# Issuing the 16 copies of the first weight sums together instead of one per weight piece

## What the kernel computes

```python
h = rmsnorm(x, norm_w)
gq, gk, gv, gg, glr, hq, hf, hi, hg = split(h @ w_in)        # w_in: 2048 x 7184
log_a = log_sigmoid(glr @ gla_w_up + gla_b_up) / 16           # glr: 16 low-rank columns
o_a = head_rmsnorm(gla(gq, gk, gv, log_a)) * silu(gg)         # 4 heads
f = lb + (1 - lb) * sigmoid(hf)
o_b = head_rmsnorm(gla(hq, 1 - f, hi, log(f))) * silu(hg)     # 8 heads
x = x + concat(o_a, o_b) @ w_out                              # w_out: 2048 x 2048
return rmsnorm(x, final_norm_w)
```

## Time and profile before

| | |
|---|---|
| median of 3 runs | 866.5 us |
| profiled execution, its own time | 865.74 us |
| its span, first to last instruction | 864.0 us |
| PE busy | 851.8 us, 99% |
| DVE / ACT / GpSimd busy | 591.8 / 424.6 / 85.1 us |
| chain that ended last | PE 89%, DVE 5%, ACT 4% |
| moved by DMA | 167.75 MB, 194 GB/s on average |
| copies of the first sums (L549) | 16, issued 37.67 to 116.6 us |
| adds of the first sums (L557) | 16, issued 122.3 us to about 200 us |

### The profile page before, as it was taken

One profiled execution on the slowest core, in us unless ns is written; L12 is line 12 of the kernel. 1 busy time (PEld: TensorE's weight loads), 2 busy tenths in 40 slices (PEclk: granted clock), 3 DMA queues, 4 the chain that ended last, 5 costly groups with the idle time before them and its releaser, 6 DMA issues.

```text
span 864.0 us, 13755 instructions
## 1 busy us (share of the span) xinstructions
PE 851.8 (99%) x5365; PEld 697.9 (81%) x5365; DVE 591.8 (68%) x949; ACT 424.6 (49%) x594; POOL 85.1 (10%) x128
## 2 busy tenths in 40 slices
PE   8999999999999999999999999999999999999996
PEld 5887888888888888888888878888888888888885
DVE  6733476653587747577887878889885678556766
ACT  7521532324444435274565665855655465335454
POOL 4110111110000001011111100000111100000000
PEclk9999999999999999999999999999999999999999
DMA  8286679988764856568776655545777987856654
GB/s 335 65 267 195 175 203 223 203 196 241 232 185 144 274 168 198 170 175 178 151 169 147 146 177 181 166 146 158 161 170 153 283 224 263 293 196 194 195 171 195
DMA packets 75459, 167.75 MB, mean 194 GB/s; under 512 B 7365, under 2 KB 15593, under 8 KB 74505
## 3 DMA queue, kind: packets, MB, share of 16 engines
q1 hardware_dynamic: 45554, 108.02, 38.2%
q0 software_dynamic: 16896, 50.34, 27.2%
q10 hardware_dynamic: 12952, 8.61, 3.4%
HBM read 158.56 MB, written 58.72 MB: 251 GB/s over the span
## 4 chain that ended last, share of the span: by engine, by line
PE 89%; DVE 5%; ACT 4%; issue 1%; ACTq 0%; DMA 0%; DVEq 0%
PE main L577 54%; PE main L837 8%; PE main L773 5%; PE sc L837 4%; PE st L837 2%; PE po L837 2%; PE sc L630 2%; PE po L658 2%; PE st L643 1%; PE st L773 1%; PE po L773 1%; PE sc L773 1%; PE po L661 1%; PE main L689 1%; DVE w_lo L1295 1%
## 5 line engine op out<-in xcount | busy, mean ns | idle before, releaser
L577 PE MATMUL main<-h_hi,w_hi 128*128 128x512 f32 x640 | 254.2, 397 | 0.1
L577 PE MATMUL main<-h_hi,w_lo 128*128 128x512 f32 x640 | 249.7, 390 | 0.0
L577 PE MATMUL main<-h_lo,w_hi 128*128 128x512 f32 x640 | 249.3, 389 | 0.0
L1295 DVE TENSOR_TENSOR w_lo<-raw,w_hi 128x1024 fp32r<-128x1024 f32 x100 | 122.1, 1221 | 113.1 <-ACT w_hi L885 112.4
L885 ACT ACTIVATE w_hi<-raw 128x1024 fp32r<-128x1024 f32 x100 | 105.7, 1058 | 180.8 <-PE main L577 135.7
L577 PEld LDWEIGHTS main<-h_hi,w_lo 128*128 128x128 f32 x640 | 120.1, 188 | 25.8
L577 PEld LDWEIGHTS main<-h_hi,w_hi 128*128 128x128 f32 x640 | 120.2, 188 | 25.5 <-issue 0.5
L577 PEld LDWEIGHTS main<-h_lo,w_hi 128*128 128x128 f32 x640 | 120.3, 188 | 23.6
L907 ACT ACTIVATE ex<-ex 128x512 f32<-128x512 f32 (+2 forms) x84 | 52.5, 641 | 23.4 <-DVE ex L1432 15.1
L577 PE MATMUL main<-w_hi,h_hi 128*128 128x512 f32 x128 | 50.9, 398 | 0.0
L1772 DVE TENSOR_TENSOR w_lo<-feat,w_hi 128x1024 fp32r<-128x1024 f32 x26 | 31.8, 1225 | 27.1 <-ACT w_hi L1218 26.9
(11 more groups left out here) (314 smaller groups left out, 1496.3 us busy)
## 6 DMA issues: line engine op xcount, KB each, us to landing
raw<-in_w_in SPq DMA_DIRECT2D x102, 512.0 KB, 4.7
w_sum<-in_w_out POOLq DMA_DIRECT2D x48, 512.0 KB, 5.3
w_sum<-in_w_in POOLq DMA_DIRECT2D x24, 512.0 KB, 5.8
w_sum<-w_sum POOLq DMA_DIRECT2D x24, 512.0 KB, 5.8
raw<-w_sum SPq DMA_DIRECT2D x24, 512.0 KB, 4.3
feat<-w_sum SPq DMA_DIRECT2D x24, 512.0 KB, 4.3
raw<-in_w_out SPq DMA_DIRECT2D x14, 512.0 KB, 5.1
feat<-in_w_out SPq DMA_DIRECT2D x10, 512.0 KB, 4.7
```

What stands on the lines that cost most here:

```text
L577: mm = pe.matmul(main[c][:, :], a, b, start=(k == 0 and j == 0), stop=(k == KT - 1 and j == 2))
L1295: dve.tensor_tensor(w_lo[:, q % SPL, :, :], (first_raw if first else raw)[:, q % RAW, :, :], w_hi[:, q % SPL, :, :], ALU.subtract).then_in ...
```

## The change

The copies of pair 2 no longer call `pace()`. Before them GpSimd waits once, until four low parts have been made (`SPL` is 4). The copies of the other pairs and all adds still call it; the counter `paced[0]` begins at 1 and is advanced by `pace()` alone.

```diff
             for pair in (2, 0, 1):
                 if pair == 0:
                     paced[0] = D_N + ND
+                if pair == 2:
+                    pool.wait_ge(lo_ok, SPL)
                 for j, (name, source) in enumerate(COPIED):
                     for q in range(QP):
-                        pace()
+                        if pair != 2:
+                            pace()
                         pool.dma_start(w_sum[pair, j, q], weight_piece(pair, source, q)).then_inc(
                             w_copied[pair * len(XS) + j], 16)
```

## The result

The median after is 880.0 us (878.62 to 880.78, five runs); before, on the same chip, 866.3 us (865.61 to 866.57). The ratio is 1.0157, 95% interval 1.0146 to 1.0167: slower by 13.7 us. The forecast was 873.3 with a range up to 879.0. The direction was right; the loss was twice the forecast and lies outside the range. Two executions behind the numbers further down, one of e2 (1063 us) and one of the kernel before beside e9 and e10 (1217 us), ran at a mean granted clock of 0.75 and 0.66 and are left out of every ratio and of e2's median.

The account below looks back on a forecast made before the run. PE was taken as the bound, so only new waits could change the time: 865.74 us of the profiled execution + 5.3 + 1.5 = 872.5, or 873.3 against the median of the runs; range 866.0 to 879.0.

Parts of the forecast that it names:

- What bounds the kernel: PE, busy 851.8 of 864.0 us; lighter DMA gives nothing back, so only making PE wait changes the time.
- The copies: GpSimd issues 16 copies from 18.9 to 29.3 us; each takes 1.5 us, with 1.3 and 1.68 as ends.
- (a): x tiles and first weights beside the copies after 20.25 us: 1.5 us of work, cover over 10 us, costs nothing.
- (b): Low-rank columns, one small packet per copy packet, land at 49.2 us; PE waits 5.3 us before piece 5, high end 7.9.
- my first rival: Same as "nothing waits": small packets go in bunches, columns land by 43.9 us, time 866.5 us; chance 0.23.
- (c): PE's clock falls to 1.2 GHz behind the wait before piece 5: costs 1.5 us, low end 0, high end 3.
- (d): Weight loads of pieces 6 and 7 after that wait, beside adds: just fit, cost nothing; high end 2.7 us.
- (e): Adds end near 120 us instead of 200, lightening a stretch where PE did not wait: gains nothing.
- nothing waits: Rival: small packets go in bunches, low-rank columns land by 43.9 us, PE unaffected, 866.5 us; chance 0.23.
- order of issue: Rival: engines serve first issued first; columns land at 35.2 us, loads of pieces 6 and 7 late, 875.3 us; chance 0.18.
- Both: Rival on slow engines: (b) at 7.9, (c) at 3, (d) at 2.7 us, giving 880 us; chance 0.04.

Follow-up runs that it names:

- e2: Changed kernel, but GpSimd starts the 16 copies only when the low-rank columns and gla_w_up have landed, adds still early: 873.2 us.
- e9: Changed kernel, but SP loads the low-rank columns ahead of the copies and the adds keep their earlier pace (pieces 17 to 32): 866.78 us.
- e10: Changed kernel, but ACT issues gla_w_up and four parameters only behind the rounding of the low-rank columns, and adds keep their earlier pace: 879.35 us.
- e11: As e10, but ACT's six issues (gla_w_up and parameters) stand further back, inside group(0, ...) at its sixth piece: 876.30 us.
- e4: Changed kernel, but the 16 adds are paced by pieces 17 to 32 as in the kernel before; copies as changed: 876.17 us.
- e8: Changed kernel, but half of the low-rank columns left out, their buffer filled by 128 runs of 512 bytes; 72 packets per DMA engine: 877.08 us.
- e3: Changed kernel, but 128 runs of 1 KB from w_in replace the 2048 of 64 bytes, low-rank columns left out; adds early: 872.29 us.

## Why the prediction was wrong

**What bounds the kernel:** right. PE was full; only new waits could change the time, and all the loss is waits and clock.

**The copies:** issued from 19.34 to 30.4 (forecast 18.9 to 29.3). In 28 to 40 us they moved 3.54 MB, 0.524 / 3.54 x 12 = 1.78 us each beside the small packets, slower than my upper end of 1.68.

**(a) x and the first weights:** nothing, right. The weight load that I put beside the columns did not go out before 50.0 in after, as PE was late.

**(b) The low-rank columns:** the mechanism held, one small packet for one large. The Trainium skill's rule ("DMA: Bandwidth & Descriptors", section "SWDGE vs HWDGE vs iDMA") of packets with up to 64 descriptors, which was my first rival, is again not what the trace shows: 894 against 971 packets in 28 to 40 us. The landing was right too, 50.5 for 49.2. It was right by parts that cancel, which is luck: the first of these packets moved near 28.9 us, not 25.0 (3.9 later), no weight load came between (1.5 less), and the 128 turns took 21.6 us where I had 22.7 with their own work (1.1 less). **The step that failed** is the path from the columns to PE: I looked only at who waits for the columns, L1031, and had PE wait 5.3 us for `w_lo` ahead of piece 5. I had not followed what else ACT issues on the same queue behind them: L1020 stood for 13.26 us, and held the transposes for 8.0 us before anyone wanted the columns. I had put down that the standing work on ACT was the high half of piece 5; it was the high parts of x, which come first. In e11, with that out of the way, (b) alone is 8.0 us against my 5.3, and 7.9 was its high end.

**(c) The clock:** right in kind, 2.0 us for 1.5, but it fell twice, the second time after a wait of only 2.1 us.

**(d) The later weight loads, "just fit", costed at nothing:** wrong by 3.8 us (e4). Landings of 8.8 and 9.5 us against the 8.3 that I took as worst. And I compared each low part with the time at which PE wants that piece, not with what stands behind it on DVE: the banks for piece 8 waited behind the low part of piece 9. The high end that I gave it, 2.7 us, was too small: four adds in 5 us are 13 us of work for all engines by the earlier trace rows, which the text noted and did not set against these loads.

**(e) Later relief:** nothing, right.

In us: forecast 5.3 + 1.5 + 0; measured 8.0 + 2.0 + 3.8, and 0.4 in small waits. The 5.3 and the 8.0 are not the same wait. Of the rivals, "nothing waits" fell with the ratio of the packets, and "order of issue" with the landing: it had the columns at 35.2 us, and they came at 50.5. The stretch that spoke for it, 124.5 to 127.5 us before, also has 87 packets of ACT's queue beside the add's 192, which the prediction did not say; so it did not show that issue order rules. "Both", which allowed for (b), (c) and (d) at their high ends at once, gave 880, with a chance of 0.04. That it has the measured time is luck: its 7.9 is the wait at piece 5, which after does not have, and its 2.7 a wait for piece 7, where PE waited for a bank. But its kind is right in this, that the terms go up together: all three hang on full DMA queues.

## What to carry to other kernels

When a burst is put in front of a queue of small descriptors, do not only ask who waits for their data; ask also what the issuing engine issues next on that queue, and what stands behind that instruction. A pacing counter that is taken from one kind of transfer changes the pace of all others that share it: price these first. For a late operand, compare its time with the next thing behind it in its engine's order, not only with its own consumer.

## What the runs showed that was not expected

- **An issue that stands.** ACT's next DMA issue on its queue took 13.26 us with 128 packets a DMA engine ahead of it and the queue hardly moving; it ended when 72 were left. With 72 queued (e8) it took 1.35 us, with 8 (e3) 0.34, with none of them (e9) 0.40. How much room an issue needs is not shown beyond these four.
- **A late start.** Behind a long queue of copies the first 64-byte packets moved about 4 us after their issue, in after and in e11 alike. What they waited for in that time, no run shows. Queues of e11 in 27 to 28 us and in 28.5 to 29 us; they were issued at 24.5:

```profile
q0 software_dynamic: 90, 0.32, 106.7%
...
q0 software_dynamic: 43, 0.16, 106.9%
q10 hardware_dynamic: 9, 0.00, 1.8%
```

- **The clock behind a short wait.** In after PE was back at 76.6 us after 2.1 us, and the granted clock (0.99 in 77 to 78 us) fell only at 78, with PE busy again, and was at 0.50 until 81. The wait of 0.5 us in the earlier trace rows had no such cost.
